# Block 1 of a two-block transformer layer on one core: the convolution of three chunks in even and odd positions, the products of the windowed attention over 64 partitions, and which engine copies and rounds what at the attention's end

## Time and profile before

| | us |
|---|---|
| median of three runs | 2324.7 (2323.81 to 2325.84) |
| the profiled execution | 2323.45 |
| its span | 2321.6 |
| TensorE busy | 2286.8 (99%) |
| VectorE busy | 1415.0 (61%) |
| ScalarE busy | 977.8 (42%) |
| GpSimd busy | 868.5 (37%) |

### The profile page before, as it was taken

One profiled execution on the slowest core, in us unless ns is written; L12 is line 12 of the kernel. 1 busy time (PEld: TensorE's weight loads), 2 busy tenths in 40 slices (PEclk: granted clock), 3 DMA queues, 4 the chain that ended last, 5 costly groups with the idle time before them and its releaser, 6 DMA issues. The chain is left out here.

```text
span 2321.6 us, 30748 instructions
## 1 busy us (share of the span) xinstructions
PE 2286.8 (99%) x11636; PEld 1919.8 (83%) x11636; DVE 1415.0 (61%) x2164; ACT 977.8 (42%) x1992; POOL 868.5 (37%) x749
## 2 busy tenths in 40 slices
PE   9999999999999999999999999999999999999998
PEld 8788878888888888888898877888888888888887
DVE  7999825955454577776533776153594545447776
ACT  4126734432323345455634755134453323234543
POOL 2000225388787800023112022121338878770003
PEclk9999999999999999999999999999999999999999
DMA  5222124233233368665002001243223323336865
GB/s 159 53 64 78 51 92 141 76 118 118 87 118 105 118 239 276 213 229 134 21 10 71 24 3 44 64 163 119 96 60 118 119 86 118 105 127 244 287 208 199
DMA packets 219590, 275.85 MB, mean 119 GB/s; under 512 B 17260, under 2 KB 144973, under 8 KB 216627
## 3 DMA queue, kind: packets, MB, share of 16 engines
q1 hardware_dynamic: 200594, 210.31, 29.0%
q10 hardware_dynamic: 18848, 63.58, 7.0%
HBM read 205.27 MB, written 68.57 MB: 118 GB/s over the span
## 5 line engine op out<-in xcount | busy, mean ns | idle before, releaser
L496 PE MATMUL P<-ah,wh 128*128 128x512 f32 (+1 forms) x1136 | 441.3, 388 | 0.5 <-POOL wl L462 0.4
L498 PE MATMUL P<-ah,wl 128*128 128x512 f32 (+1 forms) x1136 | 438.9, 386 | 0.0
L497 PE MATMUL P<-al,wh 128*128 128x512 f32 (+1 forms) x1136 | 438.6, 386 | 0.0
L496 PE MATMUL P<-wh,ah 128*128 128x512 f32 (+2 forms) x1128 | 425.9, 378 | 0.0
L498 PE MATMUL P<-wh,al 128*128 128x512 f32 (+2 forms) x1128 | 423.3, 375 | 0.0
L497 PE MATMUL P<-wl,ah 128*128 128x512 f32 (+2 forms) x1128 | 422.9, 375 | 0.0
L578 POOL TENSOR_TENSOR stats<-stats,epsc 128x1 f32<-128x1 f32 x78 | 32.5, 417 | 756.4 <-ACT xn L1892 422.3
L496 PEld LDWEIGHTS P<-ah,wh 128*128 128x128 f32 x1136 | 213.4, 188 | 44.0 <-issue 0.8
L498 PEld LDWEIGHTS P<-ah,wl 128*128 128x128 f32 x1136 | 213.4, 188 | 43.3
L497 PEld LDWEIGHTS P<-al,wh 128*128 128x128 f32 x1136 | 213.5, 188 | 42.3
L498 PEld LDWEIGHTS P<-wh,al 128*128 128x128 f32 x1128 | 212.2, 188 | 37.0
(11 more groups left out here) (372 smaller groups left out, 4263.3 us busy)
## 6 DMA issues: line engine op xcount, KB each, us to landing
rf<-ff_rows SPq DMA_DIRECT2D x154, 256.0 KB, 5.3
stage<-in_w_down_dram SPq DMA_DIRECT2D x110, 256.0 KB, 3.8
ff_rows<-sb ACTq DMA_DIRECT2D x22, 1024.0 KB, 5.2
stage<-in_w_gu_dram SPq DMA_DIRECT2D x44, 512.0 KB, 5.1
stage<-in_w_in_dram SPq DMA_DIRECT2D x22, 512.0 KB, 3.9
stage<-in_w_gate_dram SPq DMA_DIRECT2D x22, 512.0 KB, 4.1
stage<-in_w_up_dram SPq DMA_DIRECT2D x22, 512.0 KB, 5.1
ff_rows<-uo ACTq DMA_DIRECT2D x22, 512.0 KB, 3.0
```

The source lines that it names most:

```text
L496: e.matmul(out, lh, rh, start=start, stop=False, skip_group_check=onto)
L497: e.matmul(out, lh, rl, start=False, stop=False, skip_group_check=onto)
L498: return e.matmul(out, ll, rh, start=False, stop=stop, skip_group_check=onto)
```

## The change

Chunks 1 to 3 of the convolution are kept as even and odd positions side by side (`hp_split`, `acc_split`). With `xe`, `xo` the even and odd inputs and `e`, `o` the even and odd taps, three convolutions of half length are made: `e * xe` (16 instructions) into the even half of `acc`, `o * xo` (15) into a new tile `odd_taps`, and `(e + o) * (xe + xo)` (16) into the odd half; three more instructions combine them ("both", "rows", "first"). `tap_sums` holds e + o. The list takes even and odd in turn, then these three, then the 16 sums; a split instruction counts 1.1 halves. `TAPS_AT` changes: one at steps 3 to 6, three at steps 11 to 20 (of which the last takes all that is left). `conv_turn` reads one parity at a time, and the pointwise product's results are put back in the order of tokens when they are rounded (`token_order`).

The two products of `scores` run over 64 partitions each, one head's, and write to bank 0 and bank 1. kp1 needs no zeros. Each minimum signals by itself, and each exponential waits for its own. The copies of turned exponentials of steps 18, 20 and 22 go from VectorE to ScalarE, that of step 31 from ScalarE to VectorE; the norms of the convolution's last three blocks go to VectorE; the rounding to ZH of three of the first half's four channel blocks goes to VectorE; ScalarE calls silu once on a small tile at step 31.

```diff
@@ line 976 @@
     cwt = big("cwt", [128, 4, 34], 86.5)
+    hp_split = hp[:, :, :].rearrange("p c (two n) -> p c two n", two=2)
+    acc_split = acc[:, :, :].rearrange("p c (two n) -> p c two n", two=2)
+    SPLIT = (1, 2, 3)
+    odd_taps = {c: sb(f"odd_taps{c}", [128, 513], off["extra"] + 2080 * i) for i, c in enumerate(SPLIT)}
+    tap_sums = sb("tap_sums", [128, 4, 16], off["extra"] + 2080 * len(SPLIT))
@@ line 1161 @@
+    def in_turn(first, second):
...
+    def split_ops(c):
+        return in_turn([("even", c, j) for j in range(16)], [("odd", c, j) for j in range(1, 16)]) + [
+            (name, c, 0) for name in ("both", "rows", "first")] + [("sum", c, j) for j in range(16)]
     def add_taps(c):
...
+        if c in SPLIT:
+            taps[:] = in_turn(taps, split_ops(c))
+        else:
+            taps[:] = in_turn(taps, [(c, w, 512, 1024) for w in range(FIRST_HALVES)] + [
+                (c, w, 0, 1024) for w in range(FIRST_HALVES, TAPS)])
+    def split_op(name, c, j):
+        e = DV.e
+        x_even, x_odd, y_even, y_odd = hp_split[:, c, 0, :], hp_split[:, c, 1, :], acc_split[:, c, 0, :], acc_split[:, c, 1, :]
+        t_odd, bias = odd_taps[c], cwt[:, c, 31:32]
+        def behind(*names):
+            for n in names:
+                if (n, c) in split_last:
+                    DV.wait_ge(tap, split_last[n, c])
...
+        if name == "even":
+            w = cwt[:, c, 2 * j:2 * j + 1]
+            if j == 0:
+                ins = e.tensor_scalar(y_even, x_even[:, 0:512], w, None, ALU.mult)
+            else:
+                behind("even")
+                ins = e.scalar_tensor_tensor(y_even, x_even[:, j:j + 512], w, y_even, ALU.mult, ALU.add)
+        elif name == "odd":
+            w, src = cwt[:, c, 2 * j - 1:2 * j], x_odd[:, j - 1:j + 512]
+            if j == 1:
+                ins = e.tensor_scalar(t_odd[:, :], src, w, None, ALU.mult)
+            else:
+                behind("odd")
+                ins = e.scalar_tensor_tensor(t_odd[:, :], src, w, t_odd[:, :], ALU.mult, ALU.add)
+        elif name == "both":
+            behind("even", "odd")
+            ins = e.scalar_tensor_tensor(y_odd, y_even, bias, t_odd[:, 1:513], ALU.subtract, ALU.add)
+        elif name == "rows":
+            behind("even")
+            ins = e.tensor_tensor(x_even, x_even, x_odd, ALU.add)
+        elif name == "first":
+            behind("both")
+            ins = e.scalar_tensor_tensor(y_even, y_even, bias, t_odd[:, 0:512], ALU.add, ALU.add)
+        else:
+            behind("both", "rows", "sum")
+            DV.wait_ge(tap, "tap_sums")
+            ins = e.scalar_tensor_tensor(y_odd, x_even[:, j:j + 512], tap_sums[:, c, j:j + 1], y_odd, ALU.mult,
+                                         ALU.add if j else ALU.subtract)
+        ins.then_inc(*tap.up((name, c, j)))
+        split_last[name, c] = (name, c, j)
     def one_tap(c, w, a, b):
@@ line 1190 @@
     def some_taps(halves):
         while taps and halves > 0:
-            c, w, a, b = taps.pop(0)
-            one_tap(c, w, a, b)
-            halves -= (b - a) // 512
+            op = taps.pop(0)
+            if len(op) == 3:
+                split_op(*op)
+                halves -= 1.1
+            else:
+                one_tap(*op)
+                halves -= (op[3] - op[2]) // 512
@@ line 1284 @@
         def glu(c, th):
             DV.wait_ge(mm, (("u", c), 1, th))
-            e.tensor_tensor(hp[:, c, 30 + 512 * th:542 + 512 * th], P[:, u_bank(c, 1, th), :], SG[th][:, :],
-                            ALU.mult).then_inc(*ev.up(("u", c, th)))
+            if c in SPLIT:
+                e.tensor_tensor(hp_split[:, c, :, 15 + 256 * th:271 + 256 * th],
+                                P[:, u_bank(c, 1, th), :].rearrange("p (n two) -> p two n", two=2),
+                                SG[th][:, :].rearrange("p (n two) -> p two n", two=2), ALU.mult).then_inc(*ev.up(("u", c, th)))
+            else:
+                e.tensor_tensor(hp[:, c, 30 + 512 * th:542 + 512 * th], P[:, u_bank(c, 1, th), :], SG[th][:, :],
+                                ALU.mult).then_inc(*ev.up(("u", c, th)))
@@ line 1302 @@
         e.tensor_copy(cwt[:, :, :], P[:, 6, 0:136].rearrange("p (c w) -> p c w", c=4)).then_inc(*ev.up("cwt"))
+        e.tensor_copy(tap_sums[:, :, 0:1], cwt[:, :, 0:1])
+        pairs_of_taps = cwt[:, :, 1:31].rearrange("p c (j two) -> p c two j", two=2)
+        e.tensor_tensor(tap_sums[:, :, 1:16], pairs_of_taps[:, :, 0, :], pairs_of_taps[:, :, 1, :], ALU.add).then_inc(
+            *tap.up("tap_sums"))
         x_norm(6)
@@ line 1350 @@
         PL.ends("u0")
-        after(PL, "u0")
-        for g in range(2):
-            for s_ in range(2):
-                z = 64 * (1 - s_)
-                ins = PL.e.memset(kp1[z:z + 64, 2 * g + s_, :], 0.0)
-        ins.then_inc(*pz.up("kp1"))
         PL.ends("q3")
@@ line 1372 @@
     conv_at = (21, 22, 23, 24, 25, 26, 27, 28)
-    TAPS_AT = {**dict.fromkeys(range(7), 1), 12: 1, 13: 2, 14: 3, 15: 2, 16: 2, 17: 2, 18: 4, 19: 2, 20: 5}
+    TAPS_AT = {**dict.fromkeys(range(3, 7), 1), **dict.fromkeys(range(11, 21), 3)}
+    NORM_BY_DVE = 5
     def conv_step(i):
@@ line 1432 @@
         def scores(i):
             n, g = swa[i]
-            W, b = swa_width(i), i % 2
-            claim(b, mx, ("swa", i))
+            W = swa_width(i)
+            for j in range(2):
+                claim(j, mx, ("swa", i, j))
             PE.wait_ge(cp, ("q%d" % g, 0 if n < 4 else 1))
                 PE.wait_ge(cp, ("k", th))
-            PE.wait_ge(pz, "kp1")
             for j in range(2):
-                ins = e.matmul(P[:, b, 256 * j:256 * j + W], q1[:, g, 128 * n:128 * n + 128],
-                               kp1[:, 2 * (g // 2) + j, 128 * (n + 1) - W:128 * (n + 1)], start=True, stop=True)
+                ins = e.matmul(P[:, j, 0:W], q1[64 * j:64 * j + 64, g, 128 * n:128 * n + 128],
+                               kp1[64 * j:64 * j + 64, 2 * (g // 2) + j, 128 * (n + 1) - W:128 * (n + 1)], start=True,
+                               stop=True)
             ins.then_inc(*sc.up(("swa", i)))
         def turns(i):
@@ line 1470 @@
+        def conv_rows(c, tb):
+            at = 64 * (tb - tb % 2)
+            if c in SPLIT:
+                return acc_split[:, c, tb % 2, at:at + 128]
+            return acc[:, c, :].rearrange("p (n two) -> p two n", two=2)[:, tb % 2, at:at + 128]
         def conv_turn(tb):
             for c in range(4):
-                PE.wait_ge(tap, (c, TAPS - 1))
+                PE.wait_ge(tap, ("sum", c, 15) if c in SPLIT else (c, TAPS - 1))
             for c in range(4):
-                ins = e.transpose(P[:, b, 128 * c:128 * c + 128], acc[:, c, 128 * tb:128 * tb + 128], ident[:, :])
+                ins = e.transpose(P[:, b, 128 * c:128 * c + 128], conv_rows(c, tb), ident[:, :])
             ins.then_inc(*tp.up(("yc", tb)))
    @@ line 1536 @@
     def swa_on_dve(i):
-        return i % 2 == 0 and i > 16
+        return (i % 2 == 0 and i > 22) or i == N1 - 1
     def swa_pt_view(i):
@@ line 1557 @@
             rsum, esum, nm, es = swa_rows(n)[0:4]
-            AC.wait_ge(mx, ("swa", i))
             for j in range(2):
+                AC.wait_ge(mx, ("swa", i, j))
                 ins = e.activation(s[:, j, 0:W], s[:, j, 0:W], ACT.Exp, bias=nm[:, 2 * g + j:2 * g + j + 1], scale=-1.0,
@@ line 1573 @@
                 o_act(i // 4 - 2)
+            if i == N1 - 1:
+                e.activation(smalls["warm"][:, 1:2], nhalf[:, 0:1], ACT.Silu)
             if i in SEND_AT:
             for tb in conv_step(i - 3):
+                if tb >= NORM_BY_DVE:
+                    continue
                 AC.wait_ge(ro, ("yc", tb))
@@ line 1636 @@
         def maxima(i):
             n, g = swa[i]
...
@@ line 1646 @@
             for j in range(2):
-                ins = e.tensor_tensor_reduce(out=s[:, j, 0:W], in0=P[:, b, 256 * j:256 * j + W],
+                ins = e.tensor_tensor_reduce(out=s[:, j, 0:W], in0=P[:, j, 0:W],
                                              in1=b1[:, 2 * g + j, 256 - W:256], scale=1.0,
                                              accum_out=nm[:, 2 * g + j:2 * g + j + 1])
-            ins.then_inc(*mx.up(("swa", i)))
+                ins.then_inc(*mx.up(("swa", i, j)))
             if g == 3:
         def conv_stat(tb):
@@ line 1680 @@
                 conv_stat(tb)
+            for tb in conv_step(i - 3):
+                if tb >= NORM_BY_DVE:
+                    DV.wait_ge(ro, ("yc", tb))
+                    e.tensor_scalar(yc1[tb][:, :], yc1[tb][:, :], conv_cols(tb)[3], conv_cols(tb)[4], ALU.mult,
+                                    ALU.add).then_inc(*ev.up(("yn", tb)))
             if i in (7, 8):
                                        ALU.mult).then_inc(*xn.up(("mem", k)))
-            some_taps(2 * (len(taps) if i == max(TAPS_AT) else TAPS_AT.get(i, 0)))
+            some_taps(2 * len(taps) if i == max(TAPS_AT) else TAPS_AT.get(i, 0))
```

(27 more changed lines are left out.)

32 lines of the change are left out of this document (19 added, 13 removed).

## The result

| | kernel before | kernel after |
|---|---|---|
| median of 20 runs each | 2323.89 us | 2327.65 us |
| lowest and highest | 2323.43 to 2325.84 | 2322.68 to 2329.97 |
| profiled execution, span | 2323.45, 2321.6 us | 2322.68, 2320.9 us |
| mean granted clock of it | 0.999 | 0.995 |

The ratio is 1.0014 with a 95% interval of 1.0008 to 1.002: 3.3 us slower (the medians are 3.8 apart), real, but within the 0.2% that I had called no change. I forecast 2333.3, a clearly slower kernel. The median lies within the range given (2324 to 2340); the sign was right and the size was not. The times also spread over 7.3 us where the kernel before spreads over 2.4, and the profiled execution is the fastest of the 20. Three executions with a mean granted clock of 0.995 or 0.996 took 2322.7 to 2324.0 us; the other 17, at 0.994 or less, took 2326.3 to 2330.0.

What follows compares the result with a forecast made beforehand. TensorE mostly full, VectorE nearly without slack before attention; the change is worth what it moves the pointwise products' start. 9.3 + 1.4 − 1.2 − 0.5 − 0.4 = +8.6 us on 2323.45: 2332.05, median 2333.3, range 2324 to 2340.

Steps and rivals of the forecast that it cites:

- Steps 11, 12, 13 take 6, 6, 6, step 14 the last: Attention steps 11 to 14: all remaining split multiply-adds run there on VectorE, 19.6 us together, none in steps 15 to 20.
- 9.3 us: Attention steps 11 to 14: the second memory key starts at 227.3 instead of 218.00 us, +9.3 us.
- 1.33 against 1.20 us, +0.5: Attention steps 3 to 6: two half-length multiply-adds a step take 1.33 us against 1.20, +0.5 us.
- the loop of 1.27 us: First attention steps: minima, products into both banks and two handovers take 1.27 us against 1.74; three steps, −1.4 us.
- steps 0 to 10: Attention before step 11: −1.4, +0.5 and +0.2 us on a 2.2 us late start; minimum of step 11 1.5 us late.
- the clock: Case of a low granted clock: chance 0.13, with no term in the sum.
- The pair of products: Scores in steps 15 to 31: 0.95 us a pair against 0.87, +0.08 us over 17 steps, +1.4 us.
- 0.45 to 0.7 us a pair: Sign of being wrong: the scores' pair of products takes this long instead of 0.95 us from products to turns.
- the rival: Scores' products side by side in two passes: −7.5 us in place of +1.4, 2324.4 us; from 0.72 us a pair down; chance 0.20.
- the 0.055 us of the earlier trace: Chunked attention: products into separate output halves take 0.055 us each, half of 0.107 alone; evidence for the side-by-side rival.
- the 1.07 us at the first turn: Before the convolution's first turn: TensorE's wait for the last multiply-add goes, with its handover −1.2 us.
- The end: Last part, 285 to 294 us: the chain moves from ScalarE to VectorE and nothing is gained; −0.4 us in the sum.

Runs made afterwards that it cites:

- e3: Changed kernel with multiply-adds per attention step doubled (6, 6, 6 in steps 11 to 13, the rest in 14); 2337.41 us.
- e12: Kernel before with only the convolution's change (even and odd positions, its places, order of rows); 2320.98 us, ratio 0.9987.
- e10: Changed kernel with the old scores (128 partitions, one bank in turn) throughout and five multiply-adds moved to steps 18 to 20; 2318.79 us.
- e1: Changed kernel with TensorE fed unit-matrix turns behind the products of steps 0 to 3 (20, then 4 each); 2322.61 us.
- e9: Changed kernel run again, unaltered, for a second profile; the profiled execution took 2329.05 us.
- e6: Kernel before with only the end's changes (table load ahead, norms and roundings on VectorE, turned copies shifted); 2322.91 us, ratio 0.9994.
- e4: Changed kernel with the scores' products as before (128 partitions, one bank per step in turn); 2321.59 us, ratio 0.9988 to the kernel before.
- e7: Changed kernel with score products over 128 partitions, still in two banks both held per step; 2328.37 us.
- e2: Changed kernel with five half-length multiply-adds moved from the last projection step to steps 18 to 20; 2321.11 us.
- e5: Kernel before with only the scores' change (64 partitions, two banks); 2329.73 us, ratio 1.0019.
- e11: Changed kernel with five multiply-adds moved to steps 18 to 20 and TensorE fed unit-matrix turns in steps 0 to 7; 2320.21 us.

## Why the prediction was wrong

**The step that failed: how many multiply-adds run where.** "Steps 11, 12, 13 take 6, 6, 6, step 14 the last" was called the centre of the forecast, and its term, 9.3 us, is more than the whole sum of 8.6. The new line is `some_taps(2 * len(taps) if i == max(TAPS_AT) else TAPS_AT.get(i, 0))`. The 2 now belongs to the last step alone; the old line had it in front of a bracket around both. Steps 3 to 6 take 1 each, steps 11 to 17 take 3 each and step 18 the last two. The second key is 2.9 us later instead of 9.3, with 0.34 us of waiting in place of 4 or more, and e3 shows that the working behind the 9.3 was sound for the program as misread: 19.5 us measured against 19.6.

**Rightly read, my sum would have been −1.6 us, and the kernel is 3.3 slower.** The misreading stands in steps 3 to 6 as well: "1.33 against 1.20 us, +0.5" is the price of two half-length multiply-adds. One of 0.66 leaves the loop of 1.27 us as the limit, against 1.74: four times −0.47, −1.9. The minimum of step 11 would then be 2.2 − 1.4 − 1.9 + 0.2 = −0.9 us late, and the sum −0.9 + 1.4 − 1.2 − 0.5 − 0.4. That the forecast had the sign right is owed to the misreading. The minimum of step 11 was 2.2 late in the fastest execution (208.39 us, where 206.2 was the start before) and 6.6 more in the other profile. So a second step failed: steps 0 to 10, at −1.4 + 0.5 + 0.2 = −0.7 as I had them and −3.1 rightly read, against the lateness of 2.2. From the first minimum on they gained nothing in the fastest execution and lost 6.0 us in the other, whose first minimum was 0.6 later. They hold three effects, the last of which is the clock, below.
- The convolution gains. Up to step 10 there are 4 multiply-adds of half length where there were 7 full ones. A is 1.3 us shorter in e12 although VectorE starts late, and 4.5 shorter in e10, where it doesn't. I counted the saved time only for two banks, and never asked what the same steps would take with one.
- Two banks held by one step lose more than I gave them. I had the loop of minima and products at 1.27 us for width 128; measured 1.26 (182.74 to 184.00). That was right, but I set it against 1.74 for one bank with full multiply-adds between, and without those one bank takes 0.98 to 1.20 (e10). For width 256, from step 4 on, I had no such sum. It is 1.78 (e1), against 1.53 for one bank in turn (e10).

**The clock had a chance of 0.13, and no term.** The sum has nothing for a low clock in steps 0 to 10. The clock fell behind the wait in step 0, of 2.66 us. What it costs depends on the steps that it covers. From the products of step 2 to those of step 8 are 14.7 us in the first profile, and 11.9 in e1, all at 1.00: by that the 13.7 us at 0.50 cost some 2.8 us, an estimate. The 13.6 us more in e9 reach over steps 7 to 10 and make 6.4 us of time, 0.47 us each. The fastest execution of the changed kernel took 0.8 us less than the profiled one of before, and the median lies 5.0 above the fastest: the whole loss is less than what a longer fall adds. The falls came behind waits of 0.93 (e6), 1.51 (e1) and 2.66 us (the changed kernel), but the wait of 0.93 us stands in the kernel before too, with the clock at 1.00: no run shows how long a wait has to be.

**What keeps it low.** A kernel with the wide products has the clock back after 3.4 us (e4, e6, e12) or 6.8 (e7); one with the narrow products after 10.2 to 27.3 (after, e1, e2, e5, e9 and the first fall of e3), though TensorE is then busy 26.24 of 27 us (e9). e7 and the changed kernel differ in the width alone, and their mean clocks are 0.996 to 0.998 over 11 runs and 0.992 to 0.996 over 20. These mean clocks hold the stretch near 9 us too, which is 6.8 us long in e7's profile and 3.4 or 6.8 in the changed kernel's, so by the profiles the difference is not made there. That the narrow products prolong the fall is shown by this pair; why they do was not tried. The steps with memory keys, whose products are wide, have the clock at 1.00 in all of these but e3.

**The pair of products.** I took 0.95 us a pair against 0.87: three passes of 0.217, and 0.30 for the changes of shape. From products to turns are 0.63 us at the full clock, which the prediction itself had named as a sign of being wrong ("0.45 to 0.7 us a pair"). No run shows a pair in three passes; the runs show two, and in each the two products go side by side. The pair of step 10, from a timeline up to 204.3 us and one from 204.65, and the start of the same pair before, up to 201.5:

```profile
204.16 0.49 PE L1517 MATMUL P<-kp,q 64*128 64x256 f32 x2
...
204.48 0.38 PE L1517 MATMUL P<-kp,q 64*128 64x256 f32 x2
```

```profile
201.41 0.38 PE L1442 MATMUL P<-kp,q 128*128 128x256 f32 x1
```

Two records start together (6 ns apart), two more 0.32 us later, and the turns 0.31 us after these. Before, the four start one by one, 0.22 us apart. So the products do run side by side, in two passes, as the rival had it, but a pass takes 0.32 us; that three of 0.217 make nearly the same sum is chance. Why a pass is longer was not tried. In the records the next weights start to load 0.11 us behind the products' start, where before they start with it, and in both kernels the next products start 0.21 us behind their load. Where the shape changes, the weights are not loaded ahead: the load and the first product start 2 ns apart (changed kernel, 204.154 and 204.156 us; kernel before, 69.272 and 69.274).

What the change of shape costs is 0.06 at the turns and up to 0.10 ahead of the pair, together 0.78. So a step gains 0.09 where I had a loss of 0.08: the changes of shape cost 0.16 together, and I had taken 0.30, twice a bound that was itself raised from 0.09. B gives 2.4 us for 18 steps, 0.13 each, with the bank waits in it. The 0.78 lies above the 0.72 us at which I had the rival begin, and B gains 2.4 us, not its 7.5.

The overlap behind the 0.055 us of the earlier trace rows shows in the starts of its records: in the kernel before, the first two of the 20 start 7 ns apart (1147.101 and 1147.108 us), the next two 0.16 us later and every further two 0.11 us after the last, where turns of 128 columns start one by one, 0.11 us apart (201.09 to 201.31). Two passes of 0.217 us, the prediction's lower bound of 0.43 us a pair, are too low: the trace has 0.63.

**Right:** the half-length multiply-add (0.66, and 0.74 in its own chain for my 0.78); VectorE 2.2 us late at the first minimum; the 1.07 us at the first turn gone. The end I had at −0.4; in the traces C is 0.6 shorter, in e6 the time is 0.9 lower, and between e12 and e4, which differ by the end alone, nothing is gained (2320.98 and 2321.59, sets that overlap).

**The parts,** by their ratios: convolution −3.0 us (e12), the end on top of it +0.2 (e4), the scores on top of both +6.1, together +3.3. The convolution that was to be faster is; the scores take back twice as much, in steps where TensorE isn't full. Most of that is the clock: with the same scores fed to the full clock (e11) the kernel is 1.4 us above the old scores (e10), and the feeding alone costs about as much.

## What to carry to other kernels

Read a changed conditional by its brackets before working out what hangs on it: the forecast stood on the reach of one factor, and working out a step's rows from each of two readings would have cost a line. A scheme that shortens an engine's work but makes it wait for a neighbour paid here only where that engine is full: the same two-bank products gain 2.4 us in steps 13 to 31 and lose 4 to 10 in steps 0 to 12 (A of the changed kernel's two profiles against e4, the low clock in it), and using each where it fits gives 2317.16 us. When a kernel's times spread and its mean clock with them, look for one stretch at the low clock and price it with two profiles of the same kernel.

## What was not expected of the hardware

- A full queue of work at the low clock doesn't bring the clock back at once: 27 us at 0.50 with TensorE busy 26.24 us of them (e9), in steps whose scores use 64 partitions; 3.4 to 6.8 us where they use 128.
- The fall needs no long wait: in e5 it came behind waits of 0.78 and 1.25 us, and in e6 behind one of 0.93, while the profile of the kernel before has that same wait, with TensorE busy 25.28 of 30 us (180 to 210 us), at 1.00.
- Two products over 64 partitions each, in separate banks, take 0.63 us where two over 128 in one bank take 0.87 to 0.92 (256 columns, from products to turns). They start 6 ns apart, but each of their two passes takes 0.32 us, where one over 128 takes 0.22. A change between the two shapes costs 0.06 to 0.10 us.
